# Spread matmuls on fewer partitions: an identity column broadcast over 8, 16 or 32 rows instead of 128, in a two-block fp32 transformer kernel

## The chip, the cores and the metric

The kernel runs on one core of one Trainium2 chip. The metric is the device time in microseconds of one execution; several executions are timed, and their median is given. Lower is better.

## The reference

One sequence of 256 tokens of width 2048 goes through two blocks, all in fp32. The first block has an RWKV-7 mixer (16 heads of 64) beside a gated delta rule (8 value heads of 128, 4 key heads), an output projection and a gated FFN of width 5632, and ends in an RMS norm. The second has forgetting attention (16 heads of 128) and an FFN with a short causal convolution. The parts that matter here are those where one number per head and token scales or shifts a whole head:

```python
kk = l2_normalize(heads(k * k_k), RWKV_L2_EPS)                       # RWKV keys, per head
y = ((y - mean) * lax.rsqrt(var + RWKV_GN_EPS)) * ln_w + ln_b        # RWKV group norm, per head
gamma = jnp.exp(jnp.where(causal, g[..., :, None] - g[..., None, :], -jnp.inf))   # delta rule, 8 heads
k_beta = k * beta[..., None]
o = o * lax.rsqrt(jnp.mean(o * o, axis=-1, keepdims=True) + GDN_NORM_EPS) * norm_w
q = rms_norm_2(q.reshape(bsz, seq, N_HEADS, HEAD_DIM), q_gain)       # attention, 16 heads
k = rms_norm_2(k.reshape(bsz, seq, N_HEADS, HEAD_DIM), k_gain)
s = s + (cq[..., :, None] - cum[:, :, None, :])                      # forget gates, 16 heads
```

## The kernel before

Activations lie in SBUF with features on the partitions and the 256 tokens along the row. The five engines run five programs written out by hand, joined by semaphores. Most of the time goes into phases that stream weights: each weight tile is split on ScalarE (`HIW`, line 519) and VectorE (`LOW`, line 891) into a high and a low part, and TensorE runs three matmuls per tile (lines 1596 to 1598). SyncE's queue loads the weights ahead into four slots.

Between the weight phases stand the mixers. There a number per head and token lies as a row: head h on partition h (or 32 + h, 64 + h, 96 + h), tokens along the row. To use it on a whole head it is spread over the head's partitions by a matmul: the weight is one column of the identity, broadcast to as many columns as the head has rows, and the moving operand is the tile of rows. The result, in PSUM, holds row h on all these partitions. Each such fp32 matmul is recorded as two MATMULs. The spreads are:

- `head_rsqrt` (L1693): after a sum of squares (L1686), a root on ScalarE and a reciprocal on VectorE (L1036), the inverse roots in `rstd` (or `RWK`) are spread into four PSUM banks. Four calls: RWKV keys (`KSQ`, 16 matmuls on 64 output columns), delta-rule q and k (`QKSQ`, 8 matmuls; this one already takes 16 partitions of `RWK`), RWKV group norm (`RN`, 16 matmuls on 64 columns), delta-rule output norm (`GSQ`, 8 matmuls). VectorE multiplies bank by bank behind each (L1065, L1223 and L1225, L1232, L1333).
- the gates of the delta rule: `g_rows` (L1876, 8 matmuls of 256 columns from `ROWS`, read by ScalarE at L713 and VectorE at L1271) and the rows of beta (L1884, 16 matmuls of 128 columns, read at L1278).
- attention: the forget rows (L2002, 16 matmuls in 8 banks, read by three copies per bank, L1477 to L1479), and the inverse norms of q and k (L2017, 32 matmuls in 16 banks, read by 16 multiplies, L1489).

Around them, in TensorE's own order: after the key spread come the head sums (L1703, read at L1089). After the group-norm spread comes the gate product of RWKV (L1859 with 128 partitions and L1860 with 32, in turn, eight times, read bank by bank at L1246), then two transposes (L1869), `g_rows`, the beta rows. The output-norm spread is followed by a multiply (L1336) and then the output projection's weight phase. The forget rows come after the sums of squares of q and k (L1985) and a small transpose (L1992), and are followed by 32 transposes of the values (L2008, copied out by ScalarE at L835), then the q and k spread, then the attention scores (L2027, L2028).

`FW` (128 x 3 x 256) holds attention's rows: inverse norms on partitions 0 to 15 of parts 0 and 1, forget sums on partitions 96 to 127 of part 2 (`f_in = slice(96, 128)`). A spread over 128 partitions needs finite numbers in all of them, which a memset of `FW` at L1439 gives; it stands in VectorE's program in the last third of the `fox` weight phase, (g, j) = (4, 2).

Of the kernel before, what the change touches and what calls it, by code (L numbers as in the profile page):

```python
# [24 lines left out]
P = 128  # L25
T = 256
# [55 lines left out]
def build(nc, io, out):  # L82
    with ExitStack() as ctx:
# [33 lines left out]
        ident = at("ident", [P, P], o); o += 512  # L117
        ones = at("ones", [P, P], o); o += 512
        headones = at("headones", [P, P], o); o += 512
        rstd = at("rstd", [P, T], o); o += 1024  # L120
# [100 lines left out]
        ROWS = at("ROWS", [P, T], h0 + 12288)  # L221
# [23 lines left out]
        FW = at("FW", [P, 3, T], r2 + 98816)  # L245
        f_in = slice(96, 128)
# [5 lines left out]
        ps = [ctx.enter_context(nc.psum_tensor(f"ps{i}", [P, 512], F32)) for i in range(8)]  # L252
# [625 lines left out]
        def _(dve):  # L878
            V = nc.vector

            def step(ins):
                tick(ins, "dve_step")

            def settle():
                own(dve, "dve_step")
# [56 lines left out]
            for i, pack in enumerate(PACKS):  # L942
                r = sum(n for _, n in pack)
# [98 lines left out]
            for t in range(PAIRS):  # L1042
                ins = V.tensor_tensor_scan(GS[:, t, :], chunk_go[:], EG[:, t, :], 0.0, ALU.mult, ALU.add)
# [13 lines left out]
            for t in range(PAIRS):  # L1057
                c = COL["rwkv_r_k"] + t
                ins = V.scalar_tensor_tensor(TMP[:, t, :], Rf[:, t, :], vec[:, c:c + 1], Kf[:, t, :],
                                             ALU.mult, ALU.mult)  # L1060
            ins.then_inc(S("bonus_terms"), 1)
            got("bonus_terms")
            for q in range(4):
                got("hr_bc")
                ins = V.tensor_tensor(KK[:, 2 * q:2 * q + 2, :], KQ[:, 2 * q:2 * q + 2, :], pair_of(q), ALU.mult)  # L1065
# [12 lines left out]
            for t in range(PAIRS):  # L1078
# [4 lines left out]
                ins = V.tensor_scalar(a_t[:, :, 0:1], kk_t[:, :, 0:1], -1.0, None, ALU.mult)  # L1083
# [135 lines left out]
            for q in range(4):  # L1219
                got("hr_bc")  # L1220
                s2 = QKVC[:, 2 * q:2 * q + 2, :]
                if q < 2:
                    ins = V.scalar_tensor_tensor(s2, s2, float(P) ** -0.5, pair_of(4 + q), ALU.mult, ALU.mult)  # L1223
                else:
                    ins = V.tensor_tensor(s2, s2, pair_of(4 + q), ALU.mult)  # L1225
# [9 lines left out]
            for t in range(PAIRS):  # L1235
                cw, cb = COL["rwkv_ln_w"] + t, COL["rwkv_ln_b"] + t
                ins = V.tensor_scalar(BH[:, t, :], BH[:, t, :], vec[:, cw:cw + 1], vec[:, cb:cb + 1],
                                      ALU.mult, ALU.add)
# [4 lines left out]
            for q in range(4):  # L1243
                got("heads_summed")
                b2 = BH[:, 2 * q:2 * q + 2, :]
                ins = V.tensor_tensor(b2, b2, ps[q][:, :].rearrange("p (a t) -> p a t", a=2), ALU.mult)  # L1246
# [21 lines left out]
            for n in range(NT):  # L1268

                for h in range(G_HEADS):  # L1270
                    ins = V.tensor_scalar(GAM[:, 8 * n + h, :],  # L1271
                                          ps[h // 2][:, (h % 2) * T + n * P:(h % 2) * T + n * P + P],
                                          COLS[:, n, 32 + h:33 + h], 0.0, ALU.subtract, ALU.min)
# [38 lines left out]
            for c in range(NCH):  # L1312
                n, r = c // 2, slice(C * (c % 2), C * (c % 2) + C)
# [5 lines left out]
                for hb in range(2):  # L1319
                    got("gs_summed")  # L1320
                    for i in range(4):
                        h = 4 * hb + i
                        k = 4 * h + c
                        ins = V.scalar_tensor_tensor(gS[(c + 1) % 2][:, h, :], gS[c % 2][:, h, :], gdecay[:, k:k + 1],
                                                     ps[2 + hb][:, i * P:(i + 1) * P], ALU.mult, ALU.add)
# [107 lines left out]
            for g in (4, 5):  # L1433
                for j in range(2, UG + 2):
                    lo(U_FOX + g * UG + j)
                    if j == UG:
                        evac_fox(g)
                    if (g, j) == (4, 2):
                        step(V.memset(FW[:], 0.0))  # L1439
                        settle()  # L1440
                        step(V.tensor_scalar(FW[f_in, 0, :], FM[f_in, :], fox_bias, -1.0, ALU.add, ALU.mult))
                        settle()
                        step(V.tensor_scalar(FW[f_in, 1, :], FW[f_in, 0, :], -1.0, None, ALU.mult))
                        settle()
                        V.tensor_tensor(FW[f_in, 1, :], FW[f_in, 1, :], FW[f_in, 0, :], ALU.max)\
                            .then_inc(S("softplus_abs"), 1)
                        step(V.tensor_scalar(FW[f_in, 2, :], FW[f_in, 0, :], 0.0, None, ALU.max))
                    if (g, j) == (4, 4):
                        got("softplus_exp")
                        V.tensor_scalar(FW[f_in, 1, :], FW[f_in, 1, :], 1.0, None, ALU.add)\  # L1450
                            .then_inc(S("softplus_plus1"), 1)
                    if (g, j) == (4, 6):
                        got("softplus_ln")
                        step(V.tensor_tensor(FW[f_in, 0, :], FW[f_in, 1, :], FW[f_in, 2, :], ALU.add))
                        settle()
                        step(V.memset(FW[f_in, 1, :], 1.0))
                        settle()
                        V.tensor_tensor_scan(FW[f_in, 2, :], FW[f_in, 1, :], FW[f_in, 0, :], 0.0, ALU.mult, ALU.add)\
                            .then_inc(S("forget_summed"), 1)
# [113 lines left out]
        def _(pe):  # L1573
            mm = nc.tensor.matmul
# [70 lines left out]
            for n in range(NT):  # L1645
                pe.wait_ge(S(f"x_landed_{n}"), 16)
                for q in range(4):
                    for i in range(4):
                        f = 4 * q + i
                        ins = nc.tensor.transpose(ps[4 * n + q][:, i * P:(i + 1) * P], XIN[:, n, f * P:(f + 1) * P],  # L1650
                                                  ident[:])
# [4 lines left out]
            for i, pack in enumerate(PACKS):  # L1656
                r = sum(n for _, n in pack)
# [15 lines left out]
            for name, r, b0 in (("w_lora", slice(0, 64), 0), ("a_lora", slice(64, 128), 4)):  # L1673
                for t in range(PAIRS):
                    pe.wait_ge(bank_freed, N_OUT - 8 + b0 + t // 2 + 1 + FREE_BANKS)
                    ins = mm(ps[b0 + t // 2][:, (t % 2) * T:(t % 2 + 1) * T], WA_UP[r, t * P:(t + 1) * P],
                             PR[r, T_WA, PAD:TP], start=True, stop=True)
# [3 lines left out]
            def head_rsqrt(src, tiles, sel, width, buf=None, b0=0):  # L1681

                got("hr_sq")
                for f in range(tiles):
                    c = 15 - f * width - (width - 1)
                    ins = mm(ps[b0][0:16, 0:T], sel[:, c:c + 16], src[:, f, :], start=f == 0, stop=f == tiles - 1)  # L1686
                ins.then_inc(S("hr_sum"), 1)
                got("hr_inv")
                for f in range(tiles):
                    n = P // width  # L1690
                    for e in range(width):
                        h = f * width + e
                        ins = mm(ps[b0 + f // 2][e * n:(e + 1) * n, (f % 2) * T:(f % 2 + 1) * T],  # L1693
                                 ident[:, h:h + 1].broadcast_to([P, n]) if buf is None else ident[0:16, h:h + 1].broadcast_to([16, n]),
                                 rstd[:] if buf is None else buf,
                                 start=True, stop=True)
                    if f % 2:
                        ins.then_inc(S("hr_bc"), 1)
# [64 lines left out]
            for fill, kind in enumerate(FILLS):  # L1763
                if fill >= 8:
                    got(freed_by[FILLS[fill - 8]])
                dst, i = ps[fill % 8], place[kind]
# [12 lines left out]
            for lev in range(1, 6):  # L1779
                for b in range(NCH):  # L1780
# [3 lines left out]
                    for t in range(PAIRS):  # L1784
                        for rr in halves_of:
                            ins = mm(ps[2 * b][rr, t * C:(t + 1) * C], LO[rr, 8 * b + t, :], TM[rr, 8 * b + t, :],
                                     start=True, stop=True)
                    ins.then_inc(S("inv_p"), 1)
                for b in range(NCH):
                    got("inv_pm")  # L1790
                    if lev < 5:
                        for t in range(PAIRS):
                            for rr in halves_of:
                                mm(ps[2 * b][rr, t * C:(t + 1) * C], TT[rr, 8 * b + t, :], PM[rr, 8 * b + t, :],
                                   start=True, stop=True)
                    for t in range(PAIRS):
                        for rr in halves_of:
                            ins = mm(ps[2 * b + 1][rr, t * C:(t + 1) * C], PM[rr, 8 * b + t, :], TT[rr, 8 * b + t, :],
                                     start=True, stop=True)
# [73 lines left out]
            def g_rows(name):  # L1873

                for h in range(G_HEADS):
                    ins = mm(ps[h // 2][:, (h % 2) * T:(h % 2 + 1) * T],  # L1876
                             ident[:, 32 + h:33 + h].broadcast_to([P, P]), ROWS[:], start=True, stop=True)
                    if h % 2:
                        ins.then_inc(S(name), 1)
            g_rows("g_rows")  # L1880
            got("cols_made")
            for n in range(NT):
                for h in range(G_HEADS):
                    ins = mm(ps[4 + 2 * n + h // 4][:, (h % 4) * P:(h % 4 + 1) * P],  # L1884
                             ident[:, 64 + h:65 + h].broadcast_to([P, P]), ROWS[:, n * P:(n + 1) * P],
                             start=True, stop=True)
                    if h % 4 == 3:
                        ins.then_inc(S("beta_rows"), 1)
# [106 lines left out]
            for i in range(8):  # L1995
                if i == 6:
                    got("forget_cols_out")
                if i == 7:
                    got("bias_made")
                for e in range(2):  # L2000
                    r = 112 + 2 * i + e
                    ins = mm(ps[1 + i % 7][:, e * T:(e + 1) * T], ident[:, r:r + 1].broadcast_to([P, P]),  # L2002
                             FW[:, 2, :], start=True, stop=True)
                ins.then_inc(S("forget_rows"), 1)
            for i in range(8):
                got("bias_made" if i < 7 else "vt_made")
# [6 lines left out]
            for part in range(2):  # L2013
                for h in range(A_HEADS):
                    if part and h % 2 == 0:
                        got("qk_normed")
                    ins = mm(ps[h // 2][:, (h % 2) * T:(h % 2 + 1) * T], ident[:, h:h + 1].broadcast_to([P, P]),  # L2017
                             FW[:, part, :], start=True, stop=True)
                    if h % 2:
                        ins.then_inc(S("hr_bc"), 1)  # L2020
            got("qk_normed", 8)
# [65 lines left out]
```

## Time and profile before

| | us |
|---|---|
| median of 3 runs | 2731.88 (2730.34 to 2738.28) |
| the profiled execution | 2738.28 |
| its span, first to last instruction | 2736.2 |
| TensorE busy | 2590.1 (95%) |
| VectorE busy | 1494.1 (55%) |
| ScalarE busy | 1111.3 (41%) |
| mean granted TensorE clock | 0.976 |

The profiled execution is also the slowest of the three. Matmuls are pipelined, so the length of one MATMUL row is more than the distance to the next; the pace is read from successive starts. A granted clock of 1.00 is 2.4 GHz, 0.50 is 1.2 GHz.

### The profile page before, as it was taken

Reading aid. Unit: us, or ns where it says so; the run is one execution under the profiler, and the core shown is the slowest. Engines: PE = TensorE matmul, PEld = TensorE weight load, DVE = VectorE, ACT = ScalarE, POOL = GpSimd, SP = SyncE. Lnnn points to the kernel's source line nnn. Section 1 sums busy time; section 2 is a strip of 40 time slices with the busy share of each in tenths; the row PEclk is TensorE's granted clock in tenths of the full one; section 3 lists DMA queues with packets and bytes.
Section 4 is the critical chain, followed back from the end, with each engine's and each line's share of the span. In section 5 each row is a group of like instructions: output and inputs, shape, how many; then the busy total and the mean of one; then the engine's idle time right before and its main releaser. Section 6 shows DMA issues by size and latency. Waiting matters only on the chain.

```text
span 2736.2 us, 57092 instructions
## 1 busy us (share of the span) xinstructions
PE 2590.1 (95%) x24185; PEld 2525.9 (92%) x24185; DVE 1494.1 (55%) x1681; ACT 1111.3 (41%) x1051; POOL 69.2 (3%) x69
## 2 busy tenths in 40 slices
PE   6999979788999999999999799998989999999999
PEld 6999878487989999999999799977989999999999
DVE  5457556475455454444444544547467667666444
ACT  3334423332344445453333433344345555554333
POOL 1000130000100000000010000000100000000000
PEclk8999999789999999999999899999999999999999
DMA  5555200001545555555555355530545555556654
GB/s 166 195 189 197 79 3 4 1 1 63 177 149 196 188 196 189 194 191 193 194 184 167 108 192 194 189 123 17 184 154 197 186 199 185 199 186 197 190 195 154
DMA packets 169214, 421.74 MB, mean 154 GB/s; under 512 B 17462, under 2 KB 22139, under 8 KB 168859
## 3 DMA queue, kind: packets, MB, share of 16 engines
q1 hardware_dynamic: 168699, 419.13, 45.8%
q8 instruction: 76, 1.25, 0.2%
q10 hardware_dynamic: 416, 1.18, 0.1%
q14 instruction: 23, 0.19, 0.0%
HBM read 418.16 MB, written 2.10 MB: 154 GB/s over the span
## 4 chain that ended last, share of the span: by engine, by line
PE 88%; DVE 9%; ACT 2%; issue 1%; SPq 0%; DMA 0%; DVEq 0%; POOL 0%; ACTq 0%; POOLq 0%
PE ps L1596 26%; PE ps L1597 26%; PE ps L1598 26%; DVE LOW L891 1%; PE ps L1636 1%; DVE NSQ L925 1%; ACT HIW L519 1%; PE ps L1721 1%; PE ps L1731 1%; PE ps L1693 1%; PE ps L1750 1%; PE ps L1686 1%; PE ps L1728 1%; PE ps L2017 1%; PE ps L1985 1%
## 5 line engine op out<-in xcount | busy, mean ns | idle before, releaser
L891 DVE TENSOR_TENSOR LOW<-RAW,HIW 128x2048 fp32r<-128x2048 f32 (+2 forms) x400 | 909.9, 2275 | 1021.9 <-ACT HIW L519 1021.7
L1596 PE MATMUL ps<-H_ROWS,HIW 128*128 128x256 f32 x4928 | 1372.7, 279 | 43.5 <-DVE LOW L891 21.5
L1597 PE MATMUL ps<-H_ROWS,HIW 128*128 128x256 f32 x4928 | 1371.1, 278 | 0.0
L1598 PE MATMUL ps<-H_ROWS,LOW 128*128 128x256 f32 x4928 | 1370.0, 278 | 0.0
L519 ACT ACTIVATE HIW<-RAW 128x2048 fp32r<-128x2048 f32 (+2 forms) x400 | 761.0, 1903 | 1203.1 <-PE ps L1598 1202.1
L1596 PEld LDWEIGHTS ps<-H_ROWS,HIW 128*128 128x128 f32 x4928 | 932.6, 189 | 47.2 <-issue 25.8
L1598 PEld LDWEIGHTS ps<-H_ROWS,LOW 128*128 128x128 f32 x4928 | 933.4, 189 | 0.0
L1597 PEld LDWEIGHTS ps<-H_ROWS,HIW 128*128 128x128 f32 x4928 | 931.8, 189 | 0.0
L1596 PE MATMUL ps<-HID,HIW 128*128 (+1 forms) x1408 | 390.4, 277 | 1.3 <-DVE LOW L891 1.3
L1598 PE MATMUL ps<-HID,LOW 128*128 (+1 forms) x1408 | 390.3, 277 | 0.0
L1597 PE MATMUL ps<-HID,HIW 128*128 (+1 forms) x1408 | 390.3, 277 | 0.0
L1598 PEld LDWEIGHTS ps<-HID,LOW 128*128 128x128 f32 x1408 | 265.7, 189 | 0.0
L1596 PEld LDWEIGHTS ps<-HID,HIW 128*128 128x128 f32 x1408 | 264.3, 188 | 1.4 <-DVE LOW L891 1.4
L1597 PEld LDWEIGHTS ps<-HID,HIW 128*128 128x128 f32 x1408 | 264.3, 188 | 0.0
L1555 DVE SCALAR_TENSOR_TENSOR YV<-UC,vec,YV 128x256 f32<-128x256 f32 x88 | 42.1, 478 | 0.0
L1555 DVE SCALAR_TENSOR_TENSOR YG<-UC,vec,YG 128x256 f32<-128x256 f32 x88 | 42.1, 478 | 0.0
L860 ACT ACTIVATE UC<-ps 128x256 f32<-128x256 f32 x88 | 31.0, 385 | 13.4 <-PE ps L1598 13.4
L555 ACT ACTIVATE H_ROWS<-NSQ 128x512 fp32r<-128x512 f32 x32 | 20.2, 631 | 31.0 <-DVE NSQ L925 31.0
L640 ACT ACTIVATE gPM<-ps 128x512 f32<-128x512 f32 x20 | 11.9, 597 | 43.4 <-PE ps L1721 43.4
L1636 PE MATMUL ps<-NSQ,ones 128*128 128x256 f32 x96 | 25.5, 429 | 4.2 <-ACT NSQ L802 3.8
L1693 PE MATMUL ps<-rstd,ident 128*64 128x256 f32 (+1 forms) x80 | 15.7, 523 | 13.8 <-DVE rstd L1036 13.8
L1636 PEld LDWEIGHTS ps<-NSQ,ones 128*128 128x128 f32 x96 | 20.7, 219 | 8.3 <-ACT NSQ L802 4.2
(354 smaller groups left out, 1715.9 us busy)
## 6 DMA issues: line engine op xcount, KB each, us to landing
RAW<-in_ffn_w_up SPq DMA_DIRECT2D x264, 512.0 KB, 4.3
RAW<-in_ffn_w_down SPq DMA_DIRECT2D x176, 512.0 KB, 4.6
RAW<-in_w_in SPq DMA_DIRECT2D x96, 512.0 KB, 4.1
RAW<-in_fox_w_in SPq DMA_DIRECT2D x96, 512.0 KB, 4.3
RAW<-in_ffn_w_gate SPq DMA_DIRECT2D x88, 512.0 KB, 3.6
RAW<-in_w_out SPq DMA_DIRECT2D x32, 512.0 KB, 4.9
RAW<-in_fox_w_out SPq DMA_DIRECT2D x32, 512.0 KB, 5.0
RAW<-in_w_in SPq DMA_DIRECT2D x4, 576.0 KB, 4.8
```

Of the source, the lines that this page charges most:

```text
L519: A(HIW[:, u_const % 2, 0:n], RAW[:, u_const % 4, 0:n], ACT.Copy).then_inc(hi_made, 1)
L860: A(UC[:, i, 2:2 + T], ps[i][:, 0:T], ACT.Copy).then_inc(bank_freed, 1)
L891: V.tensor_tensor(LOW[:, u_const % 4, 0:n], RAW[:, u_const % 4, 0:n], HIW[:, u_const % 2, 0:n].bitcast(F32), ALU.subtract).then_inc(lo_mad ...
L925: ins = V.scalar_tensor_tensor(NSQ[:, f, :], X[:, f, :], vec[:, c + f:c + f + 1], rstd[:], ALU.mult, ALU.mult)
L1555: ins = V.scalar_tensor_tensor(y(i), UC[:, i, j:j + T], tap(g, j, i), y(i), ALU.mult, ALU.add)
L1596: mm(o_, hi_w, h_hi, start=start, stop=False)
L1597: mm(o_, hi_w, h_lo, start=False, stop=False)
L1598: i = mm(o_, lo_w, h_hi, start=False, stop=stop)
L1636: i = mm(ps[0][:, 0:T], ones[:], sq[:, f, :], start=f == (8 if presummed else 0), stop=f == KT - 1 and not presummed)
L1686: ins = mm(ps[b0][0:16, 0:T], sel[:, c:c + 16], src[:, f, :], start=f == 0, stop=f == tiles - 1)
L1693: ins = mm(ps[b0 + f // 2][e * n:(e + 1) * n, (f % 2) * T:(f % 2 + 1) * T], ident[:, h:h + 1].broadcast_to([P, n]) if buf is None else ide ...
L1721: ins = mm(ps[2 * b][:, (h % 4) * P:(h % 4 + 1) * P], LO[:, h, :], TM[:, h, :], start=True, stop=True)
```

## The change

Each spread but the one that was narrow already takes only the partitions that hold rows of its kind: 16 in `head_rsqrt`, 8 in `g_rows` (32 to 39) and in the beta rows (64 to 71), 32 in the forget rows (96 to 127), 16 in the q and k spread. Weight and moving operand are cut alike; output shapes, columns, banks, order and semaphores stay. The memset of `FW` and the wait behind it go.

```diff
                     if (g, j) == (4, 2):
-                        step(V.memset(FW[:], 0.0))
-                        settle()
                         step(V.tensor_scalar(FW[f_in, 0, :], FM[f_in, :], fox_bias, -1.0, ALU.add, ALU.mult))
...
                         ins = mm(ps[b0 + f // 2][e * n:(e + 1) * n, (f % 2) * T:(f % 2 + 1) * T],
-                                 ident[:, h:h + 1].broadcast_to([P, n]) if buf is None else ident[0:16, h:h + 1].broadcast_to([16, n]),
-                                 rstd[:] if buf is None else buf,
+                                 ident[0:16, h:h + 1].broadcast_to([16, n]), rstd[0:16] if buf is None else buf,
                                  start=True, stop=True)
...
                     ins = mm(ps[h // 2][:, (h % 2) * T:(h % 2 + 1) * T],
-                             ident[:, 32 + h:33 + h].broadcast_to([P, P]), ROWS[:], start=True, stop=True)
+                             ident[32:40, 32 + h:33 + h].broadcast_to([8, P]), ROWS[32:40, :], start=True, stop=True)
...
                     ins = mm(ps[4 + 2 * n + h // 4][:, (h % 4) * P:(h % 4 + 1) * P],
-                             ident[:, 64 + h:65 + h].broadcast_to([P, P]), ROWS[:, n * P:(n + 1) * P],
+                             ident[64:72, 64 + h:65 + h].broadcast_to([8, P]), ROWS[64:72, n * P:(n + 1) * P],
                              start=True, stop=True)
...
-                    ins = mm(ps[1 + i % 7][:, e * T:(e + 1) * T], ident[:, r:r + 1].broadcast_to([P, P]),
-                             FW[:, 2, :], start=True, stop=True)
+                    ins = mm(ps[1 + i % 7][:, e * T:(e + 1) * T], ident[f_in, r:r + 1].broadcast_to([32, P]),
+                             FW[f_in, 2, :], start=True, stop=True)
...
-                    ins = mm(ps[h // 2][:, (h % 2) * T:(h % 2 + 1) * T], ident[:, h:h + 1].broadcast_to([P, P]),
-                             FW[:, part, :], start=True, stop=True)
+                    ins = mm(ps[h // 2][:, (h % 2) * T:(h % 2 + 1) * T], ident[0:16, h:h + 1].broadcast_to([16, P]),
+                             FW[0:16, part, :], start=True, stop=True)
```

## Rows read from the trace of the kernel before

**Rows 1.** The page: the chain that ended last, by engine.
```profile
PE 88%; DVE 9%; ACT 2%; issue 1%; SPq 0%; DMA 0%; DVEq 0%; POOL 0%; ACTq 0%; POOLq 0%
```

**Rows 2.** Timeline, attention's spreads: start us, busy us, engine, line, tiles, count, idle before.
```profile
1831.66 7.17 PE L2002 MATMUL ps<-FW,ident 128*128 128x256 f32 x32
...
1835.89 3.33 DVE L1483 RECIPROCAL FW<-FW 16x512 f32<-16x512 f32 x1
...
1843.73 0.40 DVE L1479 TENSOR_TENSOR CB<-ps,causal 128x256 f32<-128x256 f32 x1
...
1846.11 14.05 PE L2017 MATMUL ps<-FW,ident 128*128 128x256 f32 x64 [0.83 <-ACT VT L835]
1847.25 13.70 DVE L1489 SCALAR_TENSOR_TENSOR QKV<-QKV,vec,ps 128x512 f32<-128x512 f32 x16 [3.12 <-PE ps L2017]
```

**Rows 3.** Windows of TensorE: stretch, length, busy (count), granted clock, DMA share, GB/s.
```profile
499.00:506.00 7.00, 6.78 (x16) 0.50 0.00 0
...
508.00:509.00 1.00, 1.00 (x4) 0.51 0.00 0
...
529.00:530.00 1.00, 1.00 (x4) 0.73 0.00 0
...
530.00:534.00 4.00, 4.00 (x9) 0.50 0.00 0
...
679.00:680.00 1.00, 0.00 (x0) 0.83 0.00 0
...
1730.00:1745.00 15.00, 15.00 (x134) 1.00 0.60 206
...
1846.00:1860.00 14.00, 13.89 (x64) 1.00 0.00 1
```

**Rows 4.** Timeline of TensorE, 499 to 545 us.
```profile
499.22 7.19 PE L1693 MATMUL ps<-RWK,ident 16*128 16x256 f32 x16 [6.65 <-DVE RWK L1036]
506.34 4.92 PE L1686 MATMUL ps<-RN,small 128*16 128x256 f32 x16
515.52 5.36 PE L1693 MATMUL ps<-rstd,ident 128*64 128x256 f32 x32 [4.27 <-DVE rstd L1036]
521.73 0.70 PE L1859 MATMUL ps<-PR,G_UP 128*128 128x256 f32 x2 [0.85 <-DVEq L1234]
522.36 0.69 PE L1860 MATMUL ps<-PR,G_UP 32*128 32x256 f32 x2
...
530.23 1.22 PE L1860 MATMUL ps<-PR,G_UP 32*128 32x256 f32 x2
531.38 1.22 PE L1859 MATMUL ps<-PR,G_UP 128*128 128x256 f32 x2
...
534.53 6.26 PE L1876 MATMUL ps<-ROWS,ident 128*128 128x256 f32 x16 [0.16 <-DVE BH L1246]
540.63 3.73 PE L1884 MATMUL ps<-ROWS,ident 128*128 128x128 f32 x32
```

**Rows 5.** Timeline of TensorE, other groups beside spreads.
```profile
318.98 6.42 PE L1676 MATMUL ps<-PR,WA_UP 64*128 64x256 f32 x32
...
335.66 6.65 PE L1693 MATMUL ps<-rstd,ident 128*64 128x256 f32 x32 [6.71 <-DVE rstd L1036]
...
670.90 3.72 PE L1693 MATMUL ps<-rstd,ident 128*128 128x256 f32 x16 [2.80 <-DVE rstd L1036]
```

**Rows 6.** Timeline of VectorE, the memset.
```profile
1738.52 0.70 DVE L1439 MEMSET FW<- 128x768 f32 x1
```

**Rows 7.** Timeline of VectorE, readers of the spreads.
```profile
342.97 2.48 DVE L1065 TENSOR_TENSOR KK<-KQ,ps 128x512 f32<-128x512 f32 x4
...
358.95 2.48 DVE L1089 TENSOR_TENSOR BON<-ps,PR 128x512 f32<-128x512 f32 x4 [0.16 <-DVE AR L1083]
...
550.30 2.47 DVE L1278 SCALAR_TENSOR_TENSOR gPM<-ps,upper 128x512 f32<-128x512 f32 x4
```

**Rows 8.** Timeline of ScalarE, the reader of `g_rows`.
```profile
539.34 2.09 ACT L713 ACTIVATE QG<-ps 128x512 f32<-128x512 f32 x4
```

## The prediction, made before the changed kernel was run

> **What bounds the kernel now.** I read the chain that ended last first: TensorE (PE) holds 88% of it [rows 1]. Most of that is the three-pass weight matmuls, which the change does not touch. The touched operations are small "spread" matmuls between the big phases. I therefore read, in this order, the timeline around each touched line (how fast a matmul follows the one before it), the granted clock in short windows of the same stretches, and who waits at the end of each stretch. The reader should see two things. TensorE runs at two levels, 2.4 GHz (clock 1.00) and 1.2 GHz (0.50). And the trace already holds two stretches with narrow matmuls, on 16 and 32 partitions, and the clock is low in both.
>
> **Pace.** Every touched matmul is recorded as two MATMULs. With 256 columns one takes 0.214 us at 2.4 GHz: VectorE's 16 multiplies behind L2017 take 13.70 us, 0.856 for each bank of four MATMULs, at clock 1.00 [rows 2, 3]. The existing 16-partition spread has 16 MATMULs from 499.22 to the start of the next group at 506.34, so 0.445 us each, clock 0.50 all through [rows 3, 4]. That is twice 0.214 (0.427 is used below) and 0.28 us over for the whole group. So at one clock a matmul on 16 partitions costs what one on 128 costs: the number of partitions buys nothing by itself, in either direction. The Trainium skill says the same and speaks against any gain here ("TensorE: Matmul & The Clock Gate", the table of its section on why this matters: a single matmul on 32 rows takes as long as one on 128, the gain is only in running several at once). Here all matmuls of a stream are cut to the same partitions, so this gives 0 for the time of the streams, as the row does.
>
> **The clock.** This is what decides. The 16-partition stream ran without a gap for 7.1 us after a pause and stayed at 1.2 GHz; then a 128-partition stream began at 506.34 and the clock rose 2.65 us later, in the window 508 to 509 [rows 3, 4]. By contrast the 128-partition stream of L1693 at 515.52 needs 5.36 us for 32 MATMULs on 64 output columns, where the one at 335.66 (low until just before its end) needs 6.65 [rows 4, 5]: the first got its clock back on the way. Second case: in the gate product L1859 (128 partitions) and L1860 (32 partitions) take turns. It starts at 2.4 GHz and, with no idle time recorded, drops in the window 529 to 530 and stays at 0.50 in 530 to 534 [rows 3, 4]. A counterexample bounds the effect: 32 MATMULs on 64 partitions at 318.98 take 6.42 us, 0.20 each, so half the rows keep 2.4 GHz [rows 5]. My reading is that narrow matmuls do not count as enough work to raise the clock, and probably not enough to hold it. That they drop a high clock is not shown by itself: in the gate product the array also pauses at each turn (0.63 us for two MATMULs against 0.427) [rows 4]. Where idle time alone drops it, it does so in 679 to 680, some 5 us after the stream at 670.90 ended [rows 3, 5]; the fall at 529 to 530 came 8 us after the turns began at 521.73. For a narrow stream I take 3 to 4 us.
>
> **The parts.**
> *The memset and its wait.* 0.70 us of VectorE at 1738.52 [rows 6] goes. TensorE is busy 15.00 of the 15 us around it [rows 3], so it hides whole: 0. Were it bare, the change would gain 0.7 to 0.8.
>
> *L1693 for the keys, 335.66.* The clock is low on entry. Narrow, it stays low to the end: 32 x 0.427 / 2 (two 64-column halves overlap, as 6.65/32 = 0.208 shows) = 6.83 instead of 6.65, ending at 342.5. Its reader on VectorE starts only at 342.97 [rows 7], so 0; with that cover gone, 0.2. The head sums behind it (8 MATMULs of 512 columns, 3.4 us at 2.4 GHz, 6.8 at 1.2) now start low, but their reader comes at 358.95 [rows 7]: 0, and at most 3.4 if nothing hid it.
>
> *L1693 for the group norm, 515.52.* All low: 6.83 for 5.36 = +1.5. VectorE multiplies bank by bank behind it and the gate product waits for that, so it is on the chain.
>
> *The gate product, unchanged itself.* Before, twelve of its sixteen groups ran at about 0.63 us and the last four at 1.15 (530.23 to 531.38) [rows 4]; it spans 521.73 to the transposes at 533.68, 11.95 us. It now follows a stream that kept the clock low, and its own mix could not even hold a high one. All low: 16 x 1.15 = 18.4, +6.45. Nothing hides it: everything behind waits for the last bank. Bounds: 0 (the clock is up again at 521.7) and +6.5. I take 6.5, because the low stretch 530 to 534 shows this same mix not raising it.
>
> *L1876 and L1884, rows of the gates, 534.53.* Before, 16 MATMULs take 6.1 us to the start of L1884 at 540.63 [rows 4]; all low 6.83, +0.7. ScalarE reads the four banks from 539.34 on, in one run of 2.09 us [rows 8], so its last read moves with the last bank: +0.7. L1884 then takes 6.8 instead of 3.73, but VectorE comes to those banks only at 550.30 [rows 7], so 0 (3.1 if bare). Each change of tile shape costs some 0.2 us, from 0.63 less 0.427; here one at entry, +0.2 at most, inside the rounding of the sum. The Trainium skill ("TensorEngine Tiling (Array Packing)", Key Properties) states such a drain when the tiling mode changes; the turns of L1859 and L1860 agree, with 0.2 us at 2.4 GHz and 0.3 at 1.2.
>
> *L1693 for the delta-rule norm, 670.90.* 3.72 us at 2.4 GHz [rows 5]; VectorE follows bank by bank and the out-projection waits for it. Bounds: 0 (clock held) and +3.4 (all low, 16 x 0.214). It comes after a pause of 2.80 us, which brings the fall nearer. I take +1.7, half.
>
> *L2002, forget rows, 1831.66.* 32 MATMULs, 7.17 us [rows 2]; all low twice that. VectorE is behind anyway: it makes three copies per bank, and a reciprocal of 3.33 us at 1835.89 stands in their middle [rows 2], so its last copy begins at 1843.73 either way. What is late is TensorE: with a fall near 1835 it ends these rows at about 1841.9 instead of 1838.8, and the 32 value transposes behind it (L2008, 128 columns, so half of 0.427 each at 1.2 GHz: 6.8 us) end near 1848.7. L2017 waits for the last copy of their banks, half a microsecond more, and starts near 1849.2 instead of 1846.11. Bounds 0 and +4; I take +3.
>
> *L2017, norm rows of q and k, 1846.11.* 64 MATMULs, 14.05 us, clock 1.00. VectorE's 16 multiplies (13.70 us) follow one for one, 0.856 each, so they wait for TensorE's four MATMULs each time [rows 2, 3]: TensorE paces. Low, a bank takes 1.71: +13.65 if low from the start, +10.3 if the transposes have raised the clock and it holds for 16 MATMULs (48 x 0.214), 0 if it holds throughout. I take +12, between the first two.
>
> *Attention scores behind it.* They would begin at 1.2 GHz and need about what the stream at 506.34 needed to rise, 2.65 us [rows 4]. Bounds 0 and +3; I take +1.
>
> **The sum:** 1.5 + 6.5 + 0.7 + 1.7 + 3 + 12 + 1 = 26.4 us. The profiled execution took 2738.28 us (span 2736.2), so 2764.7 by it. It is the slowest of the three runs shown and 6.4 above their median 2731.88; for the median I forecast 2758.3, 1.0% slower. About 0.3% (8 us) is what a measurement of this kernel can tell from no change.
>
> **Rivals.**
> *Held.* Narrow matmuls cannot raise a low clock, but do not let a high one fall. For it: no stretch of the trace has an unbroken narrow stream begun at 2.4 GHz, and the gate product pauses at its turns; half the rows held it at 318.98. Against: the gate product held it for only 8 us. Then only the stretch from 515 to 541 pays: 1.5 + 6.5 + 0.7 = 8.7, 2740.6.
> *No change.* The clock follows whether TensorE is busy, not on how many rows; the low stretch at 499 was left over from the pause before it, and the fall at 529 comes from the pauses at the turns. Then nothing moves but the hidden memset: 2731.9. For it: 7.1 us is little more than the 6 us or so that the stream at 335.66 took to rise. Against: 7.1 + 2.65 = 9.8 us of unbroken work at 1.2 GHz, against some 6 at 335.66, where the rows were full. It decides if the first spread's clock rises as before, near 341.7. The Trainium skill's own account is this one ("TensorE: Matmul & The Clock Gate", Part 1: activity releases the throttle, judged by how busy the array is, with no word of rows); by it the time would be 2731.9.
> *Faster.* A narrow matmul leaves the array sooner, and the reader paced by it gains. The place is L2017: a bank could fall from 0.856 us to what VectorE needs for a bank of this size elsewhere, 2.47/4 = 0.62 at 550.30 [rows 7]: 16 x 0.24 = -3.8; with the same for the four banks each of the two L1693 spreads on the chain, -1.9 more: 2726. It decides only if four narrow MATMULs take clearly less than 0.85 us at 2.4 GHz. Against: the equal pace above.
>
> **Chances and range.** Forecast 0.58 (its own range 2748 to 2768), held 0.18, no change 0.19, faster 0.05. The held case lies at the 0.3% bound and is split. Faster by over 0.3%: 0.04; within: 0.29; slower: 0.67. The bounds added up (4 + 13.65 + 3 + 3.4 + 8 + 0.9 = 33, and 3 of noise) give 2768 at the top. The lower end takes in the held case and stops at 2734, above most of the no-change case.
>
> **What the changed profile would show.** A low clock to the end of the stream at 335 and through 516 to 534; the gate product at 1.15 us per group throughout; L2017 at 0.427 us per MATMUL, about 27 us, with VectorE waiting for it sixteen times; value transposes at 1.2 GHz; no change in the weight phases. If L2017 still takes 14 us at clock 1.00, the forecast is wrong and the held case or no change is right; the gate product's length tells these two apart.

## The result and the profile after

The changed kernel takes 2758.9 us (median of 4 runs, 2752.64 to 2768.11) against 2731.11 us before (4 runs): ratio 1.0101, 95% interval 1.0069 to 1.0133. It is 1.0% slower; 2758.3 was forecast. The profiled execution took 2762.97 us, its span is 2761.0. Removing rows from the matmuls removed no time, and TensorE ran longer at 1.2 GHz: its mean granted clock over the span is 0.960 against 0.976. Because of removed lines, L1693 is L1691 here, the gate product is L1856 and L1857, gate and beta rows L1873 and L1881, forget rows L1999, value transposes L2005, the q and k spread L2014, scores L2024.

TensorE's timeline around the group norm and the gates, the columns as in [rows 4]:

```profile
499.01 7.19 PE L1691 MATMUL ps<-RWK,ident 16*128 16x256 f32 x16 [6.64 <-DVE RWK L1036]
506.13 6.54 PE L1684 MATMUL ps<-RN,small 128*16 128x256 f32 x16
516.94 7.09 PE L1691 MATMUL ps<-rstd,ident 16*64 16x256 f32 x32 [4.27 <-DVE rstd L1036]
524.88 1.22 PE L1856 MATMUL ps<-PR,G_UP 128*128 128x256 f32 x2 [0.85 <-DVEq L1234]
526.02 1.22 PE L1857 MATMUL ps<-PR,G_UP 32*128 32x256 f32 x2
...
542.12 1.22 PE L1857 MATMUL ps<-PR,G_UP 32*128 32x256 f32 x2
543.27 0.69 PE L1866 MATMUL ps<-ident,ROWS 128*128 128x128 f32 x2
544.12 5.91 PE L1873 MATMUL ps<-ROWS,ident 8*128 8x256 f32 x13 [0.16 <-DVE BH L1246]
549.41 0.79 PE L1881 MATMUL ps<-ROWS,ident 8*128 8x128 f32 x2
549.83 0.63 PE L1873 MATMUL ps<-ROWS,ident 8*128 8x256 f32 x1
...
561.05 1.09 PE L1891 MATMUL ps<-ident,PR 128*128 128x128 f32 x4 [4.45 <-DVE GAM L1271]
```

Around attention:

```profile
1846.68 10.69 PE L1999 MATMUL ps<-FW,ident 32*128 32x256 f32 x32
1857.31 5.16 PE L2005 MATMUL ps<-ident,QKV 128*128 128x128 f32 x32
1863.46 24.04 PE L2014 MATMUL ps<-FW,ident 16*128 16x256 f32 x64 [0.99 <-ACT VT L835]
1888.34 0.80 PE L2024 MATMUL ps<-QKV 128*128 128x128 f32 x2 [0.84 <-DVE QKV L1487]
```

TensorE's windows in both places (stretch, length, busy and count, granted clock, DMA share, GB/s):

```profile
516.00:524.00 8.00, 7.06 (x32) 0.50 0.00 0
524.00:543.00 19.00, 18.15 (x34) 0.50 0.00 0
543.00:556.00 13.00, 12.84 (x50) 0.50 0.00 1
...
1850.00:1851.00 1.00, 1.00 (x4) 0.54 0.00 0
...
1860.00:1861.00 1.00, 1.00 (x10) 0.84 0.00 0
...
1866.00:1867.00 1.00, 1.00 (x7) 1.00 0.00 0
1867.00:1868.00 1.00, 1.00 (x4) 0.57 0.00 0
1868.00:1888.00 20.00, 19.50 (x46) 0.50 0.00 0
```

The second part is the clearest picture. The forget rows begin at 1846.68 at 2.4 GHz and run without a gap; the clock falls at the start of window 1850 to 1851, some 3.4 us later. The value transposes on full rows bring it back in 1860 to 1861. The q and k spread begins at 1863.46 at 2.4 GHz, and 4 us later the clock falls again and stays low for the whole rest of the stream. L2014 takes 24.04 us where L2017 took 14.05 [rows 2], and VectorE, which was paced at 0.856 us per bank, now waits 0.96 us before a multiply of 0.75:

```profile
1870.47 0.75 DVE L1487 SCALAR_TENSOR_TENSOR QKV<-QKV,vec,ps 128x512 f32<-128x512 f32 x1 [0.96 <-PE ps L2014]
```

Cutting both spans at the same instructions shows where the time went (starts in us, from the two timelines):

| stretch | before | after | more |
|---|---|---|---|
| start to the group-norm spread | 515.52 | 516.94 | +1.4 |
| group-norm spread to the key transposes (550.53, 561.05) | 35.01 | 44.11 | +9.1 |
| to the delta-rule output norm's sums (664.48, 675.40) | 113.95 | 114.35 | +0.4 |
| sums and spread of that norm, to the projection (680.07, 696.15) | 15.59 | 20.75 | +5.2 |
| weight phases, to attention's sums (1817.52, 1832.63) | 1137.45 | 1136.48 | -1.0 |
| those sums, to the forget rows (1831.66, 1846.68) | 14.14 | 14.05 | -0.1 |
| forget rows and transposes, to the q and k spread (1846.11, 1863.46) | 14.45 | 16.78 | +2.3 |
| the q and k spread, to the scores (1861.00, 1888.34) | 14.89 | 24.88 | +10.0 |
| attention, to its projection (1902.38, 1930.05) | 41.38 | 41.71 | +0.3 |
| the rest | 833.8 | 831.0 | -2.9 |
| span | 2736.2 | 2761.0 | +24.8 |

The last row but one holds nothing that was changed; in the traces of the experiments it lies between 830.9 and 833.6, so about 3 us there belongs to no edit. Nor does the 1.4 us of the first row: the group-norm sums at 506.13 are full-row in both kernels and took 6.54 us here against 4.92 [rows 4]; the other traces with the same spread ahead have them between 4.97 and 6.51. The output norm's row is taken apart below.

### The profile page after: what moved, and what is told of

Its sections match the earlier page's. It is cut to its first block, busy times and chain, and to the rows that moved or that the text cites. A ratio compares the mean times of both kernels' runs of the same rounds, so it can differ in the third digit from the quotient of the medians.

```text
span 2761.0 us, 57091 instructions
## 1 busy us (share of the span) xinstructions
PE 2625.2 (95%) x24185; PEld 2545.1 (92%) x24185; DVE 1494.0 (54%) x1680; ACT 1111.1 (40%) x1051; POOL 69.1 (3%) x69
## 4 chain that ended last, share of the span: by engine, by line
PE 89%; DVE 8%; ACT 2%; issue 1%; SPq 0%; DMA 0%; DVEq 0%; POOL 0%; ACTq 0%; POOLq 0%
PE ps L1594 26%; PE ps L1595 25%; PE ps L1596 25%; DVE LOW L891 1%; PE ps L1634 1%; PE ps L2014 1%; DVE NSQ L925 1%; PE ps L1691 1%; ACT HIW L519 1%; PE ps L1684 1%; PE ps L1718 1%; PE ps L1728 1%; PE ps L1747 1%; PE ps L1725 1%; PE ps L1982 1%
## 5 line engine op out<-in xcount | busy, mean ns | idle before, releaser
L1691 PE MATMUL ps<-rstd,ident 16*64 16x256 f32 (+1 forms) x80 | 21.4, 634 | 13.8 <-DVE rstd L1036 13.8
L1691 PEld LDWEIGHTS ps<-rstd,ident 16*64 16x64 f32 (+1 forms) x80 | 12.2, 244 | 22.0 <-DVE rstd L1036 15.2
```

## The experiments

Each experiment names its base. Times are medians, ratios those to the kernel before on the same chip.

**Only the q and k spread narrow.**

```diff
-                    ins = mm(ps[h // 2][:, (h % 2) * T:(h % 2 + 1) * T], ident[:, h:h + 1].broadcast_to([P, P]),
-                             FW[:, part, :], start=True, stop=True)
+                    ins = mm(ps[h // 2][:, (h % 2) * T:(h % 2 + 1) * T], ident[0:16, h:h + 1].broadcast_to([16, P]),
+                             FW[0:16, part, :], start=True, stop=True)
```

> The kernel before with one part of the change: only the q and k spread (L2017) reads 16 partitions. Narrow rows let the clock fall: L2017 starts at 2.4 GHz, falls within 3 to 5 us and then takes 0.427 us per MATMUL, 24 to 25 us in all instead of 14; the scores behind it start at 1.2 GHz; 11 to 14 us slower than before. Rival, the fall in the changed kernel came from what stood ahead (the narrow forget rows), not from this stream: L2017 stays at 0.214 us and clock 1.00, no change.

2745.2 us, ratio 1.0045 (1.0027 to 1.0062), so 12 us. TensorE's timeline and windows:

```profile
1840.23 26.36 PE L2017 MATMUL ps<-FW,ident 16*128 16x256 f32 x64 [0.83 <-ACT VT L835]
```

```profile
1840.00:1841.00 1.00, 0.77 (x4) 1.00 0.00 0
1841.00:1842.00 1.00, 1.00 (x5) 0.78 0.08 16
1842.00:1867.00 25.00, 24.59 (x58) 0.50 0.00 0
```

Everything ahead of this stream is as before, pauses included, and the clock is 1.00 on entry. Behind the same pauses the full-row stream keeps 1.00 to its end [rows 2, 3]. So it is this stream's own rows that let it fall, here after some 1.3 us. The rival, a low clock inherited from the narrow forget rows, is out.

**Only the group-norm spread narrow.** `head_rsqrt` takes 16 partitions where its source is `RN`, 128 otherwise.

```diff
-                                 ident[:, h:h + 1].broadcast_to([P, n]) if buf is None else ident[0:16, h:h + 1].broadcast_to([16, n]),
-                                 rstd[:] if buf is None else buf,
+                                 ident[:, h:h + 1].broadcast_to([P, n]) if buf is None and not (src is RN) else ident[0:16, h:h + 1].broadcast_to([16, n]),
+                                 (rstd[0:16] if src is RN else rstd[:]) if buf is None else buf,
```

> The kernel before with only the group-norm spread (L1693 on rstd after RN) on 16 partitions. Narrow rows: the spread takes 6.8 us instead of 5.4, and the untouched gate product behind it 18.4 us instead of 12; the full-row gate rows behind that rise as before; 7 to 9 us slower. Rival, the gate product in the changed kernel was slow because of all the other narrow streams or by the chance of where the clock stood: it keeps at least part of its fast groups at 0.63 us, and the loss is below 3 us.

2749.24 us, ratio 1.0052 (1.0034 to 1.0071), more than expected (9 to 19 us). TensorE's timeline:

```profile
517.68 7.09 PE L1693 MATMUL ps<-rstd,ident 16*64 16x256 f32 x32 [4.27 <-DVE rstd L1036]
525.61 1.22 PE L1859 MATMUL ps<-PR,G_UP 128*128 128x256 f32 x2 [0.85 <-DVEq L1234]
...
544.01 0.69 PE L1869 MATMUL ps<-ident,ROWS 128*128 128x128 f32 x2
```

The gate product, not edited, takes 18.4 us. In the traces of the other kernels whose group-norm spread is full and whose product is unedited, it runs at about 0.63 us per group to the end and takes 10.0 us; so does this one, of the kernel with only the q and k spread narrow:

```profile
522.43 0.70 PE L1859 MATMUL ps<-PR,G_UP 128*128 128x256 f32 x2 [0.85 <-DVEq L1234]
...
531.83 0.69 PE L1860 MATMUL ps<-PR,G_UP 32*128 32x256 f32 x2
532.46 0.44 PE L1869 MATMUL ps<-ident,ROWS 128*128 128x128 f32 x2
533.30 3.72 PE L1876 MATMUL ps<-ROWS,ident 128*128 128x256 f32 x16 [0.41 <-DVE BH L1246]
```

So, with the kernel before counted in, five of six such traces hold 2.4 GHz through the product; the fall at 529 in the trace before [rows 3] was the exception. The loss against that usual case is 8.4 us for the product and about 1 for the spread, which the lower end of the interval, 9.3 us, just allows. The profiled execution, at 2741.34 us, is the fastest of five that reach 2750.65. Why the median asks for some 5 us more than the trace shows stays open.

**Only the forget rows narrow.**

```diff
-                    ins = mm(ps[1 + i % 7][:, e * T:(e + 1) * T], ident[:, r:r + 1].broadcast_to([P, P]),
-                             FW[:, 2, :], start=True, stop=True)
+                    ins = mm(ps[1 + i % 7][:, e * T:(e + 1) * T], ident[f_in, r:r + 1].broadcast_to([32, P]),
+                             FW[f_in, 2, :], start=True, stop=True)
```

> The kernel before with only the forget rows (L2002) on 32 partitions. Narrow rows: the clock falls some 3 us into the stream; the stream ends about 3 us later, the value transposes raise the clock again on their way, L2017 starts 1 to 3 us later and runs at 2.4 GHz, 14 us. Rival, 32 partitions are enough: clock 1.00 all through and L2002 at 7.2 us.

A single execution was timed, 2739.02 us, so there is no ratio to give; the reading is from its trace. TensorE's timeline and window:

```profile
1833.01 10.49 PE L2002 MATMUL ps<-FW,ident 32*128 32x256 f32 x32
1843.44 5.36 PE L2008 MATMUL ps<-ident,QKV 128*128 128x128 f32 x32
1849.78 14.05 PE L2017 MATMUL ps<-FW,ident 128*128 128x256 f32 x64 [0.99 <-ACT VT L835]
```

```profile
1836.00:1837.00 1.00, 1.00 (x6) 0.81 0.00 0
```

L2017 starts 16.77 us after the forget rows instead of 14.45, +2.3, and at full rows takes 14.05 as before. 32 partitions let the clock fall 3.6 us in, and the transposes restore it.

**The memset put back.** The changed kernel with the removed lines restored:

```diff
                     if (g, j) == (4, 2):
+                        step(V.memset(FW[:], 0.0))
+                        settle()
```

> The changed kernel with the memset of FW and its wait put back (all spreads narrow). The memset is hidden under the weight phase: as slow as the changed kernel, 1.0% over before (0.7 to 1.3%). Rival, the memset's place matters by shifting the phase of VectorE's work there: more than 2 us off the changed kernel's ratio beyond the spread of runs.

2762.93 us, ratio 1.0103 (1.0077 to 1.0129), against 1.0101 of the changed kernel. The two profiled spans are both 2761.0 us. The ratios alone, with 0.3% of uncertainty, could not tell 0.7 us from nothing; together with TensorE's 15.00 busy us of 15 around it [rows 3] they leave the memset no cost that shows.

**The other spreads narrow** (keys, gate rows, beta rows, delta-rule output norm), on the kernel before:

```diff
+                                 (rstd[0:16] if src is not RN else rstd[:]) if buf is None else buf,
...
+                             ident[32:40, 32 + h:33 + h].broadcast_to([8, P]), ROWS[32:40, :], start=True, stop=True)
...
+                             ident[64:72, 64 + h:65 + h].broadcast_to([8, P]), ROWS[64:72, n * P:(n + 1) * P],
```

> The kernel before with the spreads narrow that the other runs leave out: RWKV keys, gate rows, beta rows, delta-rule output norm. Narrow rows: keys 0, gate rows 0 to 3 us (the clock falls in them if it was high), beta rows 0 (hidden), output norm 1 to 3.4 us and up to 1 us in the projection behind it; 2 to 7 us slower, 0.1 to 0.3%. Rival, the small parts are what makes up the loss that the group norm and attention leave: over 8 us.

2737.9 us, ratio 1.0015 (0.9999 to 1.0031), so 4 us: within the 2 to 7 us expected, under the rival's 8, and not clearly apart from 0. TensorE's window in the gate rows (8 partitions), then its timeline at the output norm:

```profile
535.00:536.00 1.00, 1.00 (x4) 0.59 0.00 0
```

```profile
672.59 4.75 PE L1693 MATMUL ps<-rstd,ident 16*128 16x256 f32 x16 [2.80 <-DVE rstd L1036]
```

The gate rows begin at 534.20 at 2.4 GHz and the clock falls 1.0 us in, so 8 partitions let it fall too. In the norm's spread it fell on the way, and the spread took 4.75 us against 3.72 [rows 5]. In the changed kernel it was low from the start and the spread took 7.19. But that low start need not be the edit's: the clock fell in the pause of 2.80 us ahead of the spread, in window 682 to 683 (0.86), and it does so in four traces with full rows here too, where the spread takes 5.29. Here is the changed kernel, and one of the four, with only the forget rows narrow:

```profile
683.51 7.19 PE L1691 MATMUL ps<-rstd,ident 16*128 16x256 f32 x16 [2.80 <-DVE rstd L1036]
```

```profile
672.88 5.29 PE L1693 MATMUL ps<-rstd,ident 128*128 128x256 f32 x16 [2.80 <-DVE rstd L1036]
```

Like with like, narrow rows cost 1.0 us where the clock was high on entry (4.75 against 3.72) and 1.9 where it was low (7.19 against 5.29). The three ratios (0.45, 0.52 and 0.15%) add up to 1.12%, or 1.20% with the forget rows, whose 2.3 us are 0.08%; the whole measured 1.01%. With about 0.17% of uncertainty on each and 0.32% on the whole, that closes, though not finely enough to price a single small spread.

**The q and k spread on 64 partitions**, on the kernel before:

```diff
+                    ins = mm(ps[h // 2][:, (h % 2) * T:(h % 2 + 1) * T], ident[0:64, h:h + 1].broadcast_to([64, P]),
+                             FW[0:64, part, :], start=True, stop=True)
```

> The kernel before with only the q and k spread on 64 partitions. If what counts is how many partitions carry rows, this is the case of the 64-partition matmuls that keep 2.4 GHz: clock 1.00, L2017 at 14.05 us, within 0.2% of before. Rival, anything but the full array lets the clock fall: 24 to 26 us as with 16 partitions, 0.4 to 0.5% slower.

2729.37 us, ratio 0.9995 (0.9985 to 1.0004). TensorE's timeline and window:

```profile
1840.24 14.05 PE L2017 MATMUL ps<-FW,ident 64*128 64x256 f32 x64 [0.83 <-ACT VT L835]
```

```profile
1840.00:1855.00 15.00, 14.05 (x64) 1.00 0.00 1
```

Same place, same count, half the rows: the clock holds and nothing is lost. It is not the departure from the full array that costs, but how few partitions are left: 64 held the clock, 32 (the forget rows above) did not; nothing between was tried. Rows 16 to 63 are zeros here in both operands (the memset and the identity column), so rows that add nothing to the sum still hold the clock.

**The gate product on full rows.** On the kernel before; the added weight rows are zeros, written by GpSimd at the start.

```diff
-                ins = mm(o_, G_UP[0:32, 1, t * P:(t + 1) * P], PR[0:32, T_G1, PAD:TP], start=False, stop=True)
+                ins = mm(o_, G_UP[:, 1, t * P:(t + 1) * P], PR[:, T_G1, PAD:TP], start=False, stop=True)
...
+            for r0, r1 in ((32, 64), (64, 128)):
+                tick(nc.gpsimd.memset(G_UP[r0:r1, 1, :], 0.0), "pool_step")
+            own(pool, "pool_step")
```

> The opposite of the change, at the gate product: the kernel before, but the second factor (L1860) reads all 128 partitions instead of 32, with zeros in the added weight rows. All its matmuls then have one shape. If narrow rows and the turns between shapes cost time there, it takes 32 x 0.214 = 6.9 us at 2.4 GHz instead of 10 to 12, and the clock does not fall in it: 3 to 5 us faster (0.1 to 0.2%). Rival, the 0.63 us per matmul is the price of accumulating two products into one bank, whatever their rows: it stays, no change.

2734.5 us, ratio 0.9999 (0.9984 to 1.0014). TensorE's timeline:

```profile
523.25 0.70 PE L1862 MATMUL ps<-PR,G_UP 128*128 128x256 f32 x2 [0.85 <-DVEq L1237]
523.79 0.59 PE L1863 MATMUL ps<-PR,G_UP 128*128 128x256 f32 x2
...
530.26 0.38 PE L1872 MATMUL ps<-ident,ROWS 128*128 128x128 f32 x2
```

The product shrinks to 7.0 us: 0.43 per group, where it takes 0.63 when 128 and 32 partitions take turns. That shows the 0.2 us per turn, and rules out the accumulation as its cause. The 3 us it saves against the usual 10.0 are 0.11%, inside the interval, so the expected gain of 3 to 5 us is not shown in time.

**The same edit on the changed kernel.**

> The changed kernel with the gate product on 128 partitions. The narrow spread ahead of it leaves the clock at 1.2 GHz; a product on full rows raises it 3 to 6 us in and takes 8 to 12 us instead of 18.4, so 6 to 10 us faster than the changed kernel, 0.6 to 0.8% over before. Rival, once the clock was held low by narrow streams it stays low for this stretch whatever follows: 13.7 us, 5 us faster than the changed kernel.

2750.05 us, ratio 1.0054 (1.0033 to 1.0075), 0.5% or some 13 us below the changed kernel's ratio, more than the 6 to 10 us expected. The two kernels were not timed side by side, so this difference rests on two ratios, each with 0.2 to 0.3% of uncertainty. TensorE's timeline:

```profile
514.87 7.09 PE L1694 MATMUL ps<-rstd,ident 16*64 16x256 f32 x32 [4.27 <-DVE rstd L1039]
522.81 1.22 PE L1859 MATMUL ps<-PR,G_UP 128*128 128x256 f32 x2 [0.85 <-DVEq L1237]
...
526.38 0.83 PE L1859 MATMUL ps<-PR,G_UP 128*128 128x256 f32 x2
527.05 0.59 PE L1860 MATMUL ps<-PR,G_UP 128*128 128x256 f32 x2
...
531.80 0.38 PE L1869 MATMUL ps<-ident,ROWS 128*128 128x128 f32 x2
532.75 3.71 PE L1876 MATMUL ps<-ROWS,ident 8*128 8x256 f32 x16 [0.56 <-DVE BH L1249]
```

After the same narrow spread and the same low clock, a product on full rows brings 2.4 GHz back some 4 us in and takes 9.0 us instead of 18.4. From the spread to the key transposes it is 33.8 us (514.87 to 548.70) instead of 44.1. The make of the product decided, not what stood ahead. The edit took away the 32-partition halves and the turns between shapes at once, so which of the two keeps the mixed product from raising the clock is not separated here.

**Two narrow copies side by side**, on the kernel before. The inverse norms are copied to partitions 32 to 47, and heads take the two copies and two banks in turn.

```diff
+                    step(V.reciprocal(FW[0:16, 0:2, :], FW[0:16, 0:2, :]))
+                    settle()
+                    V.tensor_copy(FW[32:48, 0:2, :], FW[0:16, 0:2, :]).then_inc(S("hr_inv"), 1)
...
+                    h, z = i // 4 * 4 + (0, 2, 1, 3)[i % 4], 32 * (i % 2)
+                    ins = mm(ps[h // 2][:, (h % 2) * T:(h % 2 + 1) * T],
+                             ident[z:z + 16, z + h:z + h + 1].broadcast_to([16, P]),
+                             FW[z:z + 16, part, :], start=True, stop=True)
```

> The kernel before with the q and k spread narrow, but on two copies of the rows (partitions 0 to 15 and 32 to 47), taken in turn and into two banks in turn, so that two matmuls can run side by side. If narrow matmuls run side by side and each at the low clock, a pair costs one: L2017 takes some 14 us even at 1.2 GHz and VectorE still paces at 0.86 per bank; about as fast as before, within 2 us, plus 0.5 us for the copy. If the clock is held as well, VectorE becomes the pace at about 0.75 per bank: 12 us and 1 to 2 us faster. Rival, nothing runs side by side: 26 us as with one copy, or more if each turn between row groups costs 0.2 us, 0.5 to 1% slower.

2730.49 us, ratio 0.9982 (0.9969 to 0.9995). TensorE's timeline and window:

```profile
1842.61 11.85 PE L2020 MATMUL ps<-FW,ident 16*128 16x256 f32 x64 [0.83 <-ACT VT L835]
```

```profile
1845.00:1854.00 9.00, 9.00 (x45) 0.50 0.00 0
```

The clock fell here too, and still 45 MATMULs pass in 9 us, 0.20 each, where one takes 0.427 at this level: they ran in pairs. The stream takes 11.85 us instead of 14.05. VectorE's timeline shows where that came from:

```profile
1843.74 5.36 DVE L1491 SCALAR_TENSOR_TENSOR QKV<-QKV,vec,ps 128x512 f32<-128x512 f32 x8 [3.11 <-PE ps L2020]
...
1851.01 1.41 DVE L1491 SCALAR_TENSOR_TENSOR QKV<-QKV,vec,ps 128x512 f32<-128x512 f32 x2 [0.30 <-PE ps L2020]
```

The first eight banks run at VectorE's own pace, 0.67 us each, behind pairs issued at 2.4 GHz; after the fall two banks take 1.71 us, the 0.856 per bank of full rows at 2.4 GHz again. Pairs side by side are what narrow rows can buy, and the change did not collect it. The Trainium skill describes such pairs ("TensorE: Matmul & The Clock Gate", Part 3: matmuls on separate strips of rows run at the same time), and this trace agrees; that the clock falls under such a pair is in the window above.

Little of it reaches the end of the stage. From the start of the forget rows to the projection behind attention this trace takes 70.1 us (1827.53 to 1897.59), the one before 70.7 (1831.66 to 1902.38): the copy delays the transposes by 0.6 us, and the scores start at 1.2 GHz. So of the 5 us in the ratio (0.18%, outside what was expected with a low clock) some 4 have no place in the edited stage; they stay unexplained.

**Everything wide**, on the kernel before: gate product on full rows, and the delta-rule q and k spread, narrow already before the change, through `rstd` on 128 partitions.

```diff
-            head_rsqrt(QKSQ, 8, sel1, 1, RWK[0:16, 0, :], 4)
+            head_rsqrt(QKSQ, 8, sel1, 1, None, 4)
```

> The opposite of the change wherever the kernel before is narrow: gate product on 128 partitions, and the one spread that was already narrow (delta-rule q and k, through rstd) on 128 as well. If narrow rows hold the clock down, that spread raises it on its way (5 to 6 us instead of 7.1), the sums behind it start at 2.4 GHz (3.6 us instead of 5 to 6.4), and the gate product takes 7: 4 to 8 us faster than before, 0.15 to 0.3%. Rival, the clock depends on where each stretch happens to fall and not on rows: 7.1 us for the spread again, and no change in time.

2728.03 us, ratio 0.9988 (0.9979 to 0.9997), 3 us, a little less than the 4 to 8 expected. TensorE's timeline:

```profile
498.55 6.75 PE L1696 MATMUL ps<-rstd,ident 128*128 128x256 f32 x16 [6.65 <-DVE rstd L1039]
505.23 3.63 PE L1689 MATMUL ps<-RN,small 128*16 128x256 f32 x16
```

The spread gains only 0.4 us (the clock rises near its end, in 504 to 505); the sums behind it take 3.63 instead of 4.92 [rows 4], or of up to 6.54 in the other traces. The interval ends just short of 1.

**Everything wide, and the twin.** The last two edits together.

> The previous kernel and the q and k spread on two copies of 16 partitions side by side. The gains add up if they are independent: 0.2 to 0.45% faster than before (the twin alone measured 0.18%). Rival, the low clock that the twin leaves for the attention scores eats its 2 us: no faster than the previous kernel.

2727.8 us, ratio 0.9991 (0.9982 to 1.0000). Not faster than the kernel without the twin, so the gains do not add up as expected. The traces show the rival at work: from the start of the forget rows to the scores it is 28.5 us (1825.02 to 1853.51) against 29.4 without the twin (1825.50 to 1854.85), and from there to the projection 41.6 (to 1895.13) against 40.9 (to 1895.71). The scores' low clock would account for that, but kernels that enter the scores at 2.4 GHz spread from 40.8 to 41.4 there, so it is not shown apart from chance. The best versions lie 0.1 to 0.2% below the kernel before, about as much as these measurements resolve.

## Why the prediction held, point by point

- *Pace:* right. At one clock a narrow MATMUL costs the same: at 1.2 GHz 0.427 us in L2014 (a bank of four each 1.71), and at 2.4 GHz the gate rows took 3.71 us on 8 partitions and 3.72 on 128 (two of the rows above). The rival "faster" needed a quicker one, and is out.
- *The clock, not rising:* right. The gate product stayed low for 18.4 us in the changed kernel, in all three traces that have it behind a narrow spread.
- *The clock, falling:* right, and now shown in isolation: at 1850 and 1867 in gapless narrow streams begun at 2.4 GHz, and with one edit alone. The rivals "held" and "no change" are out. For "held" to be true the windows at 1850 and 1867 would read 1.00. The 3 to 4 us until the fall was a guess, since the two falls that the prediction read came 5 and 8 us on; measured were 1.0 (gate rows, 8 partitions) to 3.7.
- *Its support was partly wrong.* "Its own mix could not even hold a high one": five of six traces hold it. What the mix did not do, in three traces, is raise a low clock, and the term needed only that. In the sum it was priced against the one unlucky trace (11.95 us); against the usual 10.0 it is worth 8.4 and not 6.5.
- *Keys, 0:* right. The reader on VectorE started at 342.22, on time, and the slow head sums were hidden.
- *Group norm and gate product, 8.0, gate rows 0.7:* measured 9.1 together. The beta rows stayed hidden.
- *Delta-rule output norm, 1.7:* the pair of traces shows 5.2, but most of that is where the clock stood. With the same clock on entry narrow rows cost 1.0 or 1.9 us, so 1.7 was about right. Another 1.6 is the clock's fall in the pause ahead (5.29 against 3.72 with full rows too). The last 1.7 came from the unedited full-row sums ahead of it, 5.31 us against 3.63; the same 5.31 stands in traces of kernels with nothing narrow there. Over all traces that stretch takes 15.6 to 19.9 us with full rows (nine traces) and 18.3 to 21.7 with narrow ones (four).
- *Forget rows, 3:* 2.3. *Q and k spread, 12:* 10.0 in the changed kernel, 12.3 alone (26.36 less 14.05), as the fall came 4 us or 1 us in; the transposes did raise the clock ahead of it, and the +10.3 bound was that case. *Scores, 1:* 0.3. Two signs that the prediction named here did not show: it foresaw about 27 us for the q and k spread, and value transposes at 1.2 GHz; the stream took 24.04, and the transposes got their clock back on the way (32 in 5.16 us).
- *The memset, 0:* right as far as can be seen, by the run that puts it back.
- The sum, 26.4, against 24.8 in the span and 27.8 between the medians. The parts that belong to the edits make 23.6 (9.1, 1.9, 2.3, 10.0 and 0.3), 2.8 less than forecast; the sums ahead of both norms and the fall in the pause add 4.7, and the weight phases and the end, nothing edited in them, take off 3.9. That a forecast of 2758.3 met 2758.9 is in part luck: four executions of the changed kernel spread over 15 us.

## What to carry to other kernels

Cutting a matmul's contraction to the rows that matter saves nothing on TensorE, and a stream of 8, 16 or 32 rows can cost twice: it falls to 1.2 GHz, where it fell here 1.0 to 3.7 us in, and it leaves that clock to what follows, even to unedited work. Leave zero rows in (or pad to 64), unless the narrow matmuls are laid on separate strips of rows and banks so that they run side by side; here that made good the low clock and won under 1 us in its stage. When pricing a clock change, look at several traces of the stretch: one trace shows where the clock stood that time, and that alone moved the output norm's unedited stretch by some 4 us.

## What was not expected of the hardware

- Two narrow streams on different partitions overlap by themselves where they meet: in the changed kernel L1881 (partitions 64 to 71) starts at 549.41 before L1873 (32 to 39) has issued its last MATMULs at 549.83 and later, in the timeline above.
- Two 16-partition matmuls at once, 32 rows in use, still let the clock fall, while one on 64 partitions held it for all of 14 us.
- The delay until the clock falls in such a stream differed from run to run at the same instruction: some 1.3 us into the q and k spread in one kernel, 3.7 us in another.
- An 8-partition stream can be short enough to escape: the gate rows of the changed kernel with the full-row product took 3.71 us, at 2.4 GHz to their end.
